# Pairing the attention heads of the second block: order of transposes, array tiles and copies

## The reference, cut to what matters

```
h = rmsnorm_2(x, norm_g);  z = h @ w_in                       # 512 x 3886
b_o = dsa_mixer(dq, dk, dv, iq, ik, iw, topk=128)             # 6 heads of 64
c_o = fox_mixer(fq, fk, fv, log_sigmoid(ff + fox_bf))         # 6 heads of 64
mixed = concat([a_out * silu(pg), b_o * silu(dg), c_o * silu(fg)])
x = rmsnorm_2(x + mixed @ w_out, final_g)
```

## Time and profile before

| what | value |
|---|---|
| median of 3 runs | 1497.78 us (1497.7 to 1499.48) |
| profiled execution, span from first to last instruction | 1495.1 us |
| PE busy | 1450.1 us, 97% of the span |
| DVE, ACT, POOL busy | 821.8, 564.6, 184.3 us |
| mean granted TensorE clock over the span | 0.991 |

### The profile page before, as it was taken

How to read it: one execution, slowest core, us unless ns; L and a number is a source line. 1 busy time by engine, 2 the same in 40 slices (tenths; PEclk the granted TensorE clock), 3 DMA queues, 4 the chain that set the end, 5 groups by cost and what they waited for, 6 DMA issues and landing times.

```text
span 1495.1 us, 20211 instructions
## 1 busy us (share of the span) xinstructions
PE 1450.1 (97%) x7191; PEld 1182.8 (79%) x7191; DVE 821.8 (55%) x1399; ACT 564.6 (38%) x879; POOL 184.3 (12%) x257
## 2 busy tenths in 40 slices
PE   6899999999999999999989999999998899999998
PEld 4788888888888888888867888888886667777776
DVE  4646464746565564433446655346554688954532
ACT  4424242333424242222324443234444545545432
POOL 2001010101001010000042000000014153232300
PEclk9999999999999999999999999999999999999999
DMA  5222122221212221333322332333224212222111
GB/s 145 58 57 74 53 70 56 64 62 56 56 57 70 56 57 57 90 92 98 99 85 71 97 92 78 99 112 98 82 80 118 60 54 60 57 57 70 57 57 71
DMA packets 208501, 111.46 MB, mean 75 GB/s; under 512 B 6826, under 2 KB 206793, under 8 KB 208457
## 3 DMA queue, kind: packets, MB, share of 16 engines
q1 hardware_dynamic: 208073, 110.86, 26.0%
q0 software_dynamic: 384, 0.03, 0.0%
HBM read 108.75 MB, written 2.10 MB: 74 GB/s over the span
## 4 chain that ended last, share of the span: by engine, by line
PE 88%; DVE 8%; ACT 1%; issue 1%; POOL 0%; DMA 0%; DVEq 0%; ACTq 0%; POOLq 0%
PE gb L570 66%; PE gd L696 3%; PE gd L693 2%; PE gd L684 2%; PE gd L911 2%; PE gd L890 1%; PE gb L962 1%; PE gd L962 1%; DVE selb L1704 1%; DVE act_a L1344 1%; DVE small L1703 1%; PE gd L582 1%; PE gd L901 1%; DVE selb L1693 1%; PE gd L656 1%
## 5 line engine op out<-in xcount | busy, mean ns | idle before, releaser
L570 PE MATMUL gb<-act_a,whi 128*128 128x512 f32 x2800 | 976.2, 407 | 8.8 <-ACT act_a L985 4.5
L570 PEld LDWEIGHTS gb<-act_a,whi 128*128 128x128 f32 x2800 | 527.7, 189 | 127.7 <-issue 10.5
L570 PE MATMUL gb<-act_a,wlo 128*128 128x512 f32 x1488 | 582.2, 391 | 0.0
L570 PEld LDWEIGHTS gb<-act_a,wlo 128*128 128x128 f32 x1488 | 282.1, 190 | 55.7 <-issue 4.1
L977 ACT ACTIVATE whi<-raw 128x1024 fp32r<-128x1024 f32 x212 | 223.0, 1052 | 227.9 <-PE gb L570 198.2
L1315 DVE TENSOR_TENSOR wlo<-raw,whi 128x1024 fp32r<-128x1024 f32 x190 | 233.2, 1228 | 129.7 <-ACT whi L977 129.4
L570 PE MATMUL gb<-act_b,whi 128*128 128x512 f32 x304 | 110.4, 393 | 0.0
L1950 POOL TENSOR_TENSOR wlo<-raw,whi 128x1024 fp32r<-128x1024 f32 x22 | 52.7, 2397 | 146.1 <-ACT whi L977 146.1
L570 PEld LDWEIGHTS gb<-act_b,whi 128*128 128x128 f32 x304 | 57.0, 187 | 12.9
L1858 POOL TENSOR_TENSOR rr<-ss,eps_head 128x4 f32<-128x4 f32 x8 | 1.6, 199 | 492.9 <-DVE ss L1472 492.9
L684 PEld LDWEIGHTS gd<-Ti,LT 128*128 128x128 f32 x384 | 50.2, 191 | 4.0
(11 more groups left out here) (401 smaller groups left out, 1599.8 us busy)
## 6 DMA issues: line engine op xcount, KB each, us to landing
raw<-in_w_in_dram SPq DMA_DIRECT2D x103, 512.0 KB, 3.7
raw<-in_w_up_dram SPq DMA_DIRECT2D x44, 512.0 KB, 3.8
raw<-in_w_down_dram SPq DMA_DIRECT2D x16, 384.0 KB, 3.2
raw<-in_w_down_dram SPq DMA_DIRECT2D x16, 320.0 KB, 3.1
raw<-in_w_a_out_dram SPq DMA_DIRECT2D x8, 512.0 KB, 3.6
raw<-in_w_b_out_dram SPq DMA_DIRECT2D x8, 512.0 KB, 3.5
raw<-in_w_o_dram SPq DMA_DIRECT2D x8, 512.0 KB, 3.7
raw<-in_w_out_dram SPq DMA_DIRECT2D x8, 512.0 KB, 3.5
```

The lines of the kernel that those rows point to most:

```text
L570: ins = pe.matmul(gb[:, b, :], l, r, start=(first and m == 0), stop=(last and m == len(todo) - 1))
```

## The change

Two heads of a group are handled together. The pair g starts at slot 25 + 16g; s(c) of both heads is at start + 4c, weigh at +2, t(c) of both heads back to back at +4, pv of the pair at start + 19. Steps are numbered by `pair_step`, prob and the small columns go by step modulo 4, and s writes bank gd[t % 2]. The PV matmuls of the two heads alternate, head by head for each key block, one in the lower and one in the upper 64 output rows. For the selected heads s takes only the head's 64 rows of queries and keys, so the single-row memsets go. The even head's copy stays one instruction of ACT; the odd head's is c+1 instructions of 128x128, into four separate tiles. The scores stand four to every second slot, each on its own 32 rows (one key tile with four copies), in four banks. A few memsets of POOL go.

```diff
-        put((14 + n // 2) // 4, (14 + n // 2) % 4, ("score", n, c, h))
+        put((14 + n // 4 * 2) // 4, (14 + n // 4 * 2) % 4, ("score", n, c, h))
...
-    for t in range(2 * GROUPS):
-        start = 4 * 6 + 1 + 8 * t
+    for g in range(GROUPS):
+        start = 4 * 6 + 1 + 16 * g
         for c in range(TC):
-            todo.setdefault(start + 2 * c + 2, []).append((5, ("weigh", c, t)))
-            todo.setdefault(start + 2 * c + 4, []).append((0, ("t", c, t)))
-            todo.setdefault(start + 2 * c, []).append((3, ("s", c, t)))
-        todo.setdefault(start + 11, []).append((1, ("pv", 0, t)))
+            for t in (2 * g, 2 * g + 1):
+                todo.setdefault(start + 4 * c + 2, []).append((5, ("weigh", c, t)))
+                todo.setdefault(start + 4 * c + 4, []).append((0, ("t", c, t)))
+                todo.setdefault(start + 4 * c, []).append((3, ("s", c, t)))
+        todo.setdefault(start + 19, []).append((1, ("pv", g)))
...
+def pair_step(c, t):
+
+    return 2 * TC * (t // 2) + 2 * c + t % 2
...
-                    if n >= 2:
-                        pe.wait_ge(relu_ready, n - 1)
-                    pe.matmul(gd[:, n % 2, 0:(c + 1) * P], iq[h // 4][:, c * P:c * P + P], ikz[h % 4][:, 0:(c + 1) * P],
+                    if n >= 4:
+                        pe.wait_ge(relu_ready, n - 3)
+                    elif n >= 2:
+                        pe.wait_ge(f_rows if n == 2 else f_tok, 1)
+                    r = slice(32 * (h % 4), 32 * (h % 4) + 32)
+                    pe.matmul(gd[:, n % 4, 0:(c + 1) * P], iq[h // 4][r, c * P:c * P + P], ik4[r, 0:(c + 1) * P],
...
+                    r = slice(0, P) if g < 3 else slice(64 * i, 64 * i + 64)
+                    pe.matmul(gd[:, i, 0:(c + 1) * P], q[r, c * P:c * P + P], ring(g, 2 + i)[r, 0:(c + 1) * P],
...
-                    n = TC * t + c
+                    n = pair_step(c, t)
                     pe.wait_ge(p_ready, n + 1)
                     if n >= 1:
                         pe.wait_ge(pT_ready, n)
...
                     for j in range(TC):
-                        ins = pe.matmul(gd[64 * i:64 * i + 64, 3, j * P:T], vt[g % 2][:, j, 64 * i:64 * i + 64],
-                                        pT[:, j, j * P:T], start=(j == 0), stop=(j == TC - 1))
-                    ins.then_inc(pv_done, 1)
+                        for i in range(2):
+                            ins = pe.matmul(gd[64 * i:64 * i + 64, 3, j * P:T], vt[g % 2][:, j, 64 * i:64 * i + 64],
+                                            pTs[i][j][:, j * P:T], start=(j == 0), stop=(j == TC - 1))
+                            if j == TC - 1:
+                                ins.then_inc(pv_done, 1)
...
+                    if t % 2 == 0:
+                        sc.activation(pT[:, 0:c + 1, c * P:c * P + P],
+                                      gd[:, 2, 0:(c + 1) * P].rearrange("p (j q) -> p j q", q=P), ACT.Copy).then_inc(pT_ready, 1)
+                    else:
+                        for j in range(c + 1):
+                            ins = sc.activation(pTs[1][j][:, c * P:c * P + P], gd[:, 2, j * P:j * P + P], ACT.Copy)
+                        ins.then_inc(pT_ready, 1)
...
-                        if g in (3, 4):
-
-                            for row in (64 - 64 * i, 96 - 64 * i):
-                                dve.memset(ring(g, 2 + i)[row:row + 1, :], 0.0)
```

More of the change, by code:

```diff
@@ L116, in schedule @@
     todo = {}
[L117 to L118 removed]
+    for g in range(GROUPS):
+        start = 4 * 6 + 1 + 16 * g
         for c in range(TC):
[L120 to L126 removed]
+            for t in (2 * g, 2 * g + 1):
[3 more added lines that the diff above has]
+        todo.setdefault(start + 19, []).append((1, ("pv", g)))
+        todo.setdefault(start + (3 if g < GROUPS - 1 else 9), []).append((2, ("turn_v", g)))
     last = len(Z_UNITS)
@@ L253, in hybrid_block_kernel @@
         ot = ca
+        pTs = ([pT[:, j, :] for j in range(TC)], [flat(Ui), flat(Ti), ob[:].rearrange("p c j -> p (c j)"), pT_odd[:]])
         pvb = flat(KT)
@@ L870, in beside @@
                     else:
-                        pe.wait_ge(pT_ready, TC * 2 * g + (TC - 1 if g == GROUPS - 1 else 0))
+                        pe.wait_ge(pT_ready, TC * 2 * g + (TC if g == GROUPS - 1 else 0))
                     for c in range(TC):
@@ L897, in beside @@
                         pe.wait_ge(pT_ready, n)
-                    pe.wait_ge(v_ready, t // 2 + (0 if t == 2 * GROUPS - 2 and c < TC - 1 else 1))
+                    pe.wait_ge(v_ready, t // 2 + (0 if t >= 2 * GROUPS - 2 and c < 2 else 1))
                     for j in range(c + 1):
-                        ins = pe.transpose(gd[:, 2, j * P:j * P + P], prob[c][:, j * P:j * P + P], ident[:])
+                        ins = pe.transpose(gd[:, 2, j * P:j * P + P], prob[n % 4][:, j * P:j * P + P], ident[:])
                     ins.then_inc(p_turned, 1)
                 elif what == "pv":
-                    t = e[2]
-                    g, i = t // 2, t % 2
-                    pe.wait_ge(pT_ready, TC * (t + 1))
+                    g = e[1]
+                    pe.wait_ge(pT_ready, 2 * TC * (g + 1))
                     pe.wait_ge(v_ready, g + 1)
-                    if g and i == 0:
+                    if g:
                         pe.wait_ge(ot_ready, g)
                     for j in range(TC):
-                        ins = pe.matmul(gd[64 * i:64 * i + 64, 3, j * P:T], vt[g % 2][:, j, 64 * i:64 * i + 64],
-                                        pT[:, j, j * P:T], start=(j == 0), stop=(j == TC - 1))
-                    ins.then_inc(pv_done, 1)
+                        for i in range(2):
[3 more added lines that the diff above has]
+                                ins.then_inc(pv_done, 1)
                 elif what == "pool":
@@ L1192, in z_out @@
                     for i in range(4):
-                        sc.activation(ikz[i][32 * i:32 * i + 32, :], src[0:32, :], ACT.Copy)
+                        sc.activation(ik4[32 * i:32 * i + 32, :], src[0:32, :], ACT.Copy)
                     sc.activation(flat(iwff), src, ACT.Copy).then_inc(z_read, 1)
@@ L1244, in beside @@
                     sc.wait_ge(score_done, n + 1)
-                    sc.activation(relu[n % 2][:, 0:(c + 1) * P], gd[:, n % 2, 0:(c + 1) * P], ACT.Relu).then_inc(relu_ready, 1)
+                    sc.activation(relu[n % 2][:, 0:(c + 1) * P], gd[:, n % 4, 0:(c + 1) * P], ACT.Relu).then_inc(relu_ready, 1)
                 elif what == "turn_v":
@@ L1262, in beside @@
                     w = (c + 1) * P
-                    sc.activation(prob[c][:, 0:w], gd[:, c % 2, 0:w], ACT.Exp, bias=small[:, 8 + c:9 + c], scale=-1.0,
-                                  accum_out=small[:, 12 + c:13 + c]).then_inc(exp_ready, 1)
+                    k = n % 4
+                    sc.activation(prob[k][:, 0:w], gd[:, t % 2, 0:w], ACT.Exp, bias=small[:, 8 + k:9 + k], scale=-1.0,
+                                  accum_out=small[:, 12 + k:13 + k]).then_inc(exp_ready, 1)
                 elif what == "t":
                     _, c, t = e
-                    n = TC * t + c
+                    n = pair_step(c, t)
                     sc.wait_ge(p_turned, n + 1)
[L1269 to L1272, removed]
+                    if t >= 2 and c == 0:
+                        sc.wait_ge(pv_done, t // 2 * 2)
+                    if t % 2 == 0:
[5 more added lines that the diff above has]
+                        ins.then_inc(pT_ready, 1)
                 elif what == "pv":
-                    t = e[2]
-                    if t % 2:
-                        mixed(t // 2, (5, 6, 7, 2, 3, 4)[t // 2])
+                    mixed(e[1], (5, 6, 7, 2, 3, 4)[e[1]])
             for u in range(len(Z_UNITS)):
@@ L1730, in beside @@
                 elif what == "pv":
[L1731 to L1739, removed]
+                    g = e[1]
+                    dve.wait_ge(pv_done, 2 * g + 2)
+                    dve.wait_ge(z_read, G_READ[g])
+                    if g:
+                        dve.wait_ge(m_lo, g)
+                    dve.tensor_tensor(ot[:], gd[:, 3, :], sg[g % 2][:], ALU.mult).then_inc(ot_ready, 1)
+                    low(g, (5, 6, 7, 2, 3, 4)[g])
             def low(i, k):
@@ L1889, in _ @@
             pool.wait_ge(out_read, R_D)
-            for i in range(4):
-                ins = pool.memset(ikz[i], 0.0)
-            link(ins)
+            pool.wait_ge(xr_ready, 2)
             for g in range(2):
```

28 lines of the change are left out of this document (15 added, 13 removed).

## The result

The changed kernel is slower: a median of 1519.94 us (1519.34 to 1523.31, 4 runs) against 1497.85, ratio 1.0144 with a 95% interval of 1.013 to 1.0157. Its profiled span is 1517.9 us against 1495.1 before, so both comparisons give 22 to 23 us. The forecast was 1511 with a range of 1497 to 1526; the narrower range of its favoured rival A, 1504 to 1519, is missed by about 1 us.

A forecast was written before the change was run, and what follows sets the result against it. DVE bounds the score stage, PE nearly all the rest. Terms +27.7 + 1.7 - 1.2 - 11.2 - 0.7 - 0.2 - 2.5 = +13.6 took the span from 1495.1 to 1508.7, median 1511 us; range 1497 to 1526.

The forecast's parts named there:

- rival A: Whole kernel: the prediction's own sum, with waits on gd[2] and partial matmul overlap, 1511 us, own range 1504 to 1519; 55%.
- 27.7 us: Second transposing event of each pair waits for ACT's copy out of gd[2]: +27.7 us, bounds 18.8 and 27.7.
- The sign for a late pair: Distance between pv events of late pairs was to rise from 34.25 to 36.8 us in the trace after.
- PV: -11.2: Alternating PV matmuls of two heads overlap in start order, a pair 2.73 against 4.60 us: -11.2, bounds 0 and -13.8.
- an overlap better than three of four: Sign against the prediction: PE makes up the waits by matmuls overlapping better than three matmul times for four.
- Selected heads' products: net -0.2: s matmuls on 64 rows: -3.2 from overlap, +3.0 from 12 array form changes, net -0.2; bounds +3.0 and -6.4.
- Scores: -2.5: Score stage: DVE's work unchanged, four scores in flight let it wait less; -2.5 us, half of bounds 0 to -5.1.
- Clock: +1.7: One drop of PE's clock to half speed after the longer waits at c = 0: +1.7 us, bounds 0 and 10.
- the -1.2 of DVE's lead: Stretch through the 512-wide top-k rounds, where DVE leads by 1.2 us and hides that much of PE's waits: -1.2.
- B (no overlap): fp32 matmuls in different array parts don't overlap, so PV and products give back nothing: 1526 us; 20%.
- C: Overlap complete (PV -13.8, products -6.4), DVE's score waits all go (-5.1), no clock loss: 1498 us, no change; 11%.
- D: Complete overlap and ACT free at t(0), so waits are only 18.8 us: 1489, faster; 14%, including anything not thought of.

The follow-up runs named there:

- first two experiments: Changed kernel with the odd head's t(c) one slot later, 1494.88 us (ratio 0.9974); then two slots later, values turned between the last group's c = 1 events, 1492.68 us (0.9956).

## Why the prediction was right, and which terms were off

The forecast's cause was right: the second transposing event waits for ACT to empty gd[2], and these waits cost more than the array tiles give. The term was 27.7 us, the trace has 26.9, and taking the waits away alone (first two experiments) turned 1519.9 into 1494.9 and 1492.7. The six at c = 0 are 1.47 to 2.82 us; four of them 1.92, where ACT's row of five instructions had given 1.96, and the last 2.82 for 2.83. The sign for a late pair, 36.8 us, came out as 35.49 at full clock, because the overlap was better than forecast, and as 37.05 and 37.48 with a drop.

PV: -11.2 was taken, from the assumption that records start in order and a matmul's two records lie behind each other. The step that failed is that order: record one of both heads starts together, and a pair takes 2.30 us, not 2.73. The gain is 6 x 2.30 = 13.8, the bound that was kept for full overlap. The prediction had named an overlap better than three of four as a sign against it; it came, but did not make up the waits. The experiment without alternation confirms 1.56 of the 2.30 a pair; the rest is read from the rows.

Selected heads' products: net -0.2 was forecast, -1.9 is what the pair with all rows shows. Overlap is full (a pair of 512-wide products takes 1.06 us, one alone 0.86), and what is lost around the products is 0.40 a pair, not 0.25.

Scores: -2.5 was forecast, the stage became 0.8 us longer. PE's part is done (a group of four 256-wide products takes 0.64 us), but the statement that DVE's work is unchanged failed: DVE is busy 30.17 us in place of 28.04. With two scores to a slot again it is 28.26, so the two more come with the four to every second slot. The run with POOL late shows that POOL slows DVE's instructions; how the plan by four makes them meet more often was not followed up. The clock, 0.94 in this stage and 1.00 before, is no cause: it was 0.88 in the kernel with the odd t(c) two slots later, and the stage as long (33.95).

Clock: +1.7 was forecast, one drop. The two drops in the last two pairs cost 1.55 each by experiment. The lines of the seven stretches have more of them: the stretches of groups 1 and 2 are at 0.92 and 0.96, that is 41.74 x 0.08 + 39.27 x 0.04 = 4.9 us of PE's full-speed time at most, since PE also waits in some of it (group 0 is left out; its stretch has a drop in both kernels, as the earlier trace rows show for before). The largest loss, in group 1, follows a wait that the forecast did not have, one for DVE:

```profile
1295.57 1.11 PE L912 MATMUL gd<-ident,Yb 128*128 128x128 f32 x4 [2.54 <-DVE Yb L1745]
```

For the six microseconds behind it, 1295.50 to 1301.50, the granted clock is 0.50. And the stretch behind the last pv grew by 1.68 us (63.78 against 62.10 to the end), with a drop among its matmuls in this run and none in the kernel before; runs with and without such a drop show 63.8 and 62.1. With the two late ones (3.1) that makes up to 9.7 us, inside the bound of 10 but more than five times the value taken. This is the mis-sized term that weighs most: up to 8.0 of the 9.2 us by which the span exceeds 1508.7. The scores (3.3) come next, and the larger gains of PV (2.6) and of the products (1.7) hide a part of both: that the forecast came so near is in part luck.

The sum with measured terms: waits 26.9, clock 9.7, scores 0.8, less PV 13.8 and products 1.9, is +21.7. The first score also stands 1.1 us later than before (1190.05 against 1188.94), ahead of all that was changed in the plan; in the other runs it lies between 1189.5 and 1192.9. So it is spread from one execution to the next: already at 20 to 40 us, in the block that the change does not touch, the clock was 0.74 here and 0.83 before. Together 22.8, as much as the spans differ. It fits better than its terms are known, the clock's above all: the -1.2 of DVE's lead and the -0.7 of the last copy are not in it, and neither are PE's new waits for DVE, the 2.54 above and 1.16 in group 2.

Of the rivals, B (no overlap) is excluded by the rows, the complete overlap of C and D is what happened, but with the waits of A, with changes of form that are not free and with drops of the clock. The rule of the Trainium skill that several tiles take one matmul's time (TensorE: Matmul & The Clock Gate, Part 3) is borne out for PV, where a pair took 2.30 us, one head's time.

## What to carry to other kernels

Before two events of a kind are put side by side on an in-order engine to make their matmuls overlap, look for what they share: a single PSUM bank that another engine must empty turns neighbours into a round trip, 0.7 to 0.9 us here and 2 where that engine has a queue of its own. Separate the part that gains from neighbourhood (the products) from the part that loses by it (the transposes); one or two slots for one event made a kernel 1.4% slower than before into one 0.3 to 0.4% faster. A saving on the matrix engine counts only in stages where it leads, and a wait of some 2 us there can cost 1.5 us more by the clock. And before work is moved off one engine's way, look at what it will then lie beside: with POOL's start moved behind two thirds of the scores, DVE was busy 5.5 us less beside them and 8.0 us more right after.

## What the runs showed of the hardware

**float32 matmuls in different parts of the array run together in full.** Column halves: 2.30 us for two heads. Row quarters: four products of 256 columns take 0.64 us (1190.05 to 1190.69) and four of 384 columns 0.86 (1197.23 to 1198.09), where one alone takes 0.43 and 0.64 by the rate of the earlier trace rows: one product's time and 0.21 to 0.22 more.

**Some of DVE's instructions stand still beside one of POOL.** Timeline of the changed kernel, DVE and then POOL:

```profile
1282.16 0.42 DVE L1745 TENSOR_SCALAR qc<-qc,small 128x384 f32<-128x384 f32 x1
1282.68 2.57 DVE L1745 TENSOR_SCALAR kc<-kc,small 128x384 f32<-128x384 f32 x1
...
1282.67 2.37 POOL L1960 TENSOR_TENSOR wlo<-raw,whi 128x1024 fp32r<-128x1024 f32 x1 [5.55 <-ACT whi L989]
```

The same operation takes 0.42 us, and 2.57 when it starts with a POOL split; it ends 0.2 after it. DVE again, and POOL, ten microseconds later:

```profile
1293.21 0.68 DVE L1720 MATCH_REPLACE8 selb<-small,selb 128x512 f32<-128x512 f32 x1
...
1294.12 1.40 DVE L1745 TENSOR_SCALAR Yb<-Yb,small 128x512 f32<-128x512 f32 x1
...
1295.62 0.49 DVE L1745 TENSOR_SCALAR zs<-zs,small 128x512 f32<-128x512 f32 x1
...
1292.89 2.35 POOL L1960 TENSOR_TENSOR wlo<-raw,whi 128x1024 fp32r<-128x1024 f32 x1 [7.85 <-ACT whi L989]
```

The top-k replacement inside the split's time takes its usual 0.68 us; the division takes 1.40 in place of 0.49 and ends 0.3 behind the split. PE's wait of 2.54 us in group 1 was for this division. After the 2.57 us of the first case PE's second event of that slot waited 0.83 us for this very result instead of for ACT.

**The clock after waits of similar length.** After the wait of 1.73 us at 1350.51 the clock stayed full (35.49 at 1.00), after one of the same 1.73 us at 1386.01 it fell, to a mean of 0.57 over the four microseconds that follow:

```profile
1387.00:1391.00 4.00, 4.00 (x11) 3.17 (x12) 1.78 (x8) 1.94 (x5) 0.00 (x0) 0.57 0.00 0
```

Of the four waits of 1.73 us at c = 0 two are followed by a drop (1311.30, 1386.01) and two by full clock (1269.56, 1350.51). Which of them is can't be told from the length alone in these traces, so a forecast can price one drop, and only bound their number.
